# Streaming-encoder layer with PEER on one core: expert weights kept in PSUM by halves of a down tile, a row block's norm spread over the next block's rows, the second pair's first tile computed in one go

## The reference

```python
# e_idx, gates: (1024 tokens, 8 heads, 16 chosen experts)
def block(args):
    hb, eb, gb = args
    u = jnp.take(expert_down, eb, axis=0)
    act = jax.nn.gelu(jnp.einsum('td,thkd->thk', hb, u))
    wv = gb * act
    vv = jnp.take(expert_up, eb, axis=0)
    return jnp.einsum('thk,thkd->td', wv, vv)
x = x + peer_layer(...)
out = rms_norm(x, g_final)
```

## Time and profile before

| what | value |
|---|---|
| median of 3 runs | 2916.48 us (2912.46 to 2918.59) |
| the profiled execution | 2923.75 us |
| its span, first to last instruction | 2921.7 us |
| mean granted PE clock over the span | 0.984 |
| stage with the expert pairs, from the span's start | about 1127 us to the end |
| PE busy in the span | 2785.8 us |
| DVE busy in the span | 2406.7 us |
| POOL busy in the span | 2116.6 us |
| ACT busy in the span | 935.6 us |
| moved by DMA | 717.87 MB |

### The profile page before, as it was taken

How to read it: one execution, slowest core, us unless ns; L and a number is a source line. 1 busy time by engine, 2 the same in 40 slices (tenths; PEclk the granted TensorE clock), 3 DMA queues, 4 the chain that set the end, 5 groups by cost and what they waited for, 6 DMA issues and landing times.

```text
span 2921.7 us, 39464 instructions
## 1 busy us (share of the span) xinstructions
PE 2785.8 (95%) x14843; PEld 2420.2 (83%) x14843; DVE 2406.7 (82%) x4433; ACT 935.6 (32%) x1366; POOL 2116.6 (72%) x1542
## 2 busy tenths in 40 slices
PE   8999999989997999999999999999999999999995
PEld 6688777677887888889989988999888889988995
DVE  2622797654799995889999999998999999999998
ACT  4422443323322995222222222222222222222222
POOL 5444477385686997788778886888777688878885
PEclk9999999999998999999999999999999999999998
DMA  4123422123322778889989988999889799989996
GB/s 154 49 87 99 162 61 84 44 87 108 104 90 102 236 234 283 314 327 349 337 310 352 348 307 322 346 337 351 313 318 344 283 347 346 329 317 348 337 343 218
DMA packets 267725, 717.87 MB, mean 246 GB/s; under 512 B 20880, under 2 KB 104208, under 8 KB 267536
## 3 DMA queue, kind: packets, MB, share of 16 engines
q0 software_dynamic: 110912, 403.75, 36.8%
q1 hardware_dynamic: 156624, 311.61, 31.7%
HBM read 657.86 MB, written 57.41 MB: 245 GB/s over the span
## 4 chain that ended last, share of the span: by engine, by line
DVE 20%; PE 20%; DMA 7%; issue 7%; POOL 5%; ACT 1%; DVEq 0%; POOLq 0%; SPq 0%; ACTq 0%
DVE acc L1883 9%; DVE e_y L1939 4%; DMA up<-in_down,e_idx 4%; PE ybank L1728 3%; PE abank L1712 3%; PE abank L1713 3%; PE abank L1714 3%; PE ybank L1729 3%; PE ybank L1730 3%; DVE up L1871 3%; DMA up<-in_up,e_idx 3%; POOL tdown_lo L1660 2%; DVE w_lo L1932 2%; POOL up L1653 2%; DVE w L1928 2%
## 5 line engine op out<-in xcount | busy, mean ns | idle before, releaser
L1712 PE MATMUL abank<-m_hT,tdown_hi 128*128 128x384 f32 (+1 forms) x1856 | 577.3, 311 | 4.7 <-PEq L1359 2.5
L1714 PE MATMUL abank<-m_hT,tdown_lo 128*128 128x384 f32 (+1 forms) x1856 | 577.5, 311 | 0.0
L1713 PE MATMUL abank<-m_hlo,tdown_hi 128*128 128x384 f32 (+1 forms) x1856 | 576.7, 311 | 0.0
L1728 PE MATMUL ybank<-tup_hi,w_hi 128*128 128x512 f32 x1280 | 506.8, 396 | 46.4 <-DVE e_y L1939 29.0
L941 POOL TENSOR_TENSOR m_wlo<-m_raw,m_whi 128x1024 fp32r<-128x1024 f32 x128 | 312.4, 2448 | 306.7 <-ACT m_whi L719 303.2
L1883 DVE SCALAR_TENSOR_TENSOR acc<-up,e_act,acc 128x1024 f32<-128x1024 f32 x381 | 489.5, 1285 | 43.7 <-DMA up<-in_up,e_idx 16.4
L1871 DVE CUSTOM_DVE_ANT_0 up<-up,acc 128x1024 f32<-128x1024 f32 x384 | 453.1, 1212 | 71.7 <-DMA up<-in_down,e_idx 62.4
L1729 PE MATMUL ybank<-tup_lo,w_hi 128*128 128x512 f32 x1280 | 504.5, 394 | 0.0
L1730 PE MATMUL ybank<-tup_hi,w_lo 128*128 128x512 f32 x1280 | 504.1, 394 | 0.0
L1653 POOL DMA_INDIRECT up<-in_up,e_idx x384 | 396.6, 1033 | 106.7 <-issue 88.9
L1653 POOL DMA_INDIRECT up<-in_down,e_idx x384 | 402.3, 1048 | 98.0 <-issue 73.7
(11 more groups left out here) (241 smaller groups left out, 4566.9 us busy)
## 6 DMA issues: line engine op xcount, KB each, us to landing
e_tup<-in_up SPq DMA_DIRECT2D x128, 512.0 KB
m_raw<-in_tiles SPq DMA_DIRECT2D x116, 512.0 KB, 3.5
e_tdown<-in_downT SPq DMA_DIRECT2D x116, 512.0 KB
gates<-all_table SPq DMA_DIRECT2D x64, 640.0 KB
all_table<-t_out SPq DMA_DIRECT2D x9, 4096.0 KB, 14.7
m_raw<-in_downT SPq DMA_DIRECT2D x12, 512.0 KB, 3.7
up<-in_down,e_idx POOLq DMA_INDIRECT x384
up<-in_up,e_idx POOLq DMA_INDIRECT x384
```

The source lines that it names most:

```text
L1712: nc.tensor.matmul(out, tdown_hi[:, q, at], h2T_hi[:, k, a:b], start=k == 0, stop=False)
L1713: nc.tensor.matmul(out, tdown_hi[:, q, at], h2T_lo[:, a:b, at], start=False, stop=False)
L1714: ins = nc.tensor.matmul(out, tdown_lo[:, q, at], h2T_hi[:, k, a:b], start=False, stop=k == KD - 1)
L1728: nc.tensor.matmul(out, w_hi[r][:, q, ts], tup_hi[r][:, q, ds], start=q == 0, stop=False)
```

## The change

Four things, all in the expert stage.

1. **Weights in PSUM, by halves.** For all pairs but the first, gelu writes back into `abank`, the gates are multiplied there, and `w_hi` and `w_lo` are made from there. `expert_gelu`, `weights`, `weights_high` and `weights_rest` each take one half (256 or 384 columns) at a time: twice as many instructions. A half of `abank` is then free only after `weights_rest`, so `down_half` waits on `w_low` of the same half of the tile before. The queues of ACT and DVE are written anew around the halves. Of the tiles made ahead, gelu reads `w` and writes `abank`.
2. **The tiles made ahead are loaded early.** `w` is used by nothing else now, so `load_pre` waits for the gelu of the tiles made ahead before (ten pairs back), not for `w_low` of the pair before.
3. **The norm of a gathered block, spread.** After the block's last row DVE does only `x2 += acc` and the sum of squares; the mean goes behind the next row, the root on ACT behind 3 rows, the reciprocal behind 5, the scaling behind 7. The third block's norm stays in one piece. The sum of squares writes its products into the row's own slot of the ring, not into `acc`.
4. **First pairs.** down(1,0,0) and down(1,0,1) both stand before up(0,0); up(0,1) has no down tile ahead of it.

The diff, cut to its core:

```diff
+def halves(p, q, half=1):
+    return 2 * (2 * p + q) + half + 1
...
+        def down_out(half):
+            return abank[:, half, 0:(SPLIT[half][1] - SPLIT[half][0]) * P]
+        def weight_place(p, q, half):
+            return down_out(half) if p else w[:, q, SPLIT[half][0] * P:SPLIT[half][1] * P]
...
             def load_pre(p, q):
-                sp.wait_ge(w_low, 2 * (p - 1) + q + 1)
+                read = PRE.index(p) and PRE[PRE.index(p) - 1]
+                sp.wait_ge(gl_ready if read else w_low, halves(read, q))
...
                 if half == 0:
                     pe.wait_ge(down_low, 2 * normal(p) + q + 1)
-                    if q:
-                        pe.wait_ge(gl_ready, 2 * p + 1)
-                    elif p:
-                        pe.wait_ge(gl_ready, 2 * (p - 2 if p - 1 in PRE else p - 1) + 2)
+                if (p, q) == (0, 1) or (p, q) == (1, 0):
+                    pe.wait_ge(gl_ready, halves(0, 1 - q, half))
+                elif p:
+                    pe.wait_ge(w_low, halves(p, q, half) - 2)
...
-                    if p + 1 < NPAIR and t < 4:
+                    if p == 0 and t == 0:
+                        for half in range(2):
+                            down_half(1, 0, half)
+                    elif p + 1 < NPAIR and t < 4 and (p, t) != (0, 1):
                         down_half(p + 1, t // 2, t % 2)
                     up_product(p, t)
...
-                for half, (a, b) in enumerate(SPLIT):
-                    ins = nc.scalar.activation(w[:, q, a * P:b * P], abank[:, half, 0:(b - a) * P], ACT.Gelu_apprx_tanh)
-                ins.then_inc(gl_ready, 1)
+                    act.wait_ge(a_ready, halves(normal(p), q, half))
+                nc.scalar.activation(dst, src, ACT.Gelu_apprx_tanh).then_inc(gl_ready, 1)
...
+                a, b, c, d, e = parts(rows_of_pair(p), (2, 3, 3, 1, 1))
+                up_high_of(p + 1, 0)
+                expert_gelu(p + 1, 0, 0)
                 row_events(a)
+                weights_high(p + 1, 0, 0)
+                row_events(b)
+                expert_gelu(p + 1, 0, 1)
                 if p + 2 < NPAIR:
                     down_high_of(p + 2, 0)
+                up_high_of(p + 1, 1)
+                weights_high(p + 1, 0, 1)
...
+            def row_and_norm(n):
+                row(n)
+                for b in range(DB - 1):
+                    since = n - row_at("up", b, NSEL - 1)
+                    if since == VAR_BEHIND:
+                        dve.wait_ge(row_used, row_at("up", b, NSEL - 1) + 1)
+                        norm_start(slice(ND, ND + 1))
+                    if since == RINV_BEHIND:
+                        norm_root(b, slice(ND, ND + 1))
+                    if since == APPLY_BEHIND:
+                        apply_block(b)
...
-                by = w[:, q].rearrange("p (c t) -> p c t", t=TC)
-                nc.vector.tensor_tensor(by, by, gates[p % 2][:, :, q], ALU.mult).then_inc(w_ready, 1)
+                by = weight_place(p, q, half).rearrange("p (c t) -> p c t", t=TC)
+                nc.vector.tensor_tensor(by, by, gates[p % 2][:, a * P // TC:b * P // TC, q], ALU.mult).then_inc(w_ready, 1)
...
-                a, b, c, d, e = parts(rows_of_pair(p), (3, 2, 1, 3, 1))
+                a, b, c, d, e, f, g = parts(rows_of_pair(p), (2, 1, 2, 1, 2, 1, 1))
```

More of the change, by code:

```diff
@@ L1434 @@
 RU = 8
+VAR_BEHIND, ROOT_BEHIND, RINV_BEHIND, APPLY_BEHIND = 1, 3, 5, 7
 LAST_ROOTS = ((0, 1, 2), (3, 4))
@@ L1714, in down_half @@
                     ins = nc.tensor.matmul(out, tdown_lo[:, q, at], h2T_hi[:, k, a:b], start=False, stop=k == KD - 1)
-                if half == 1:
-                    ins.then_inc(a_ready, 1)
+                ins.then_inc(a_ready, 1)
             def up_product(p, t):
                 if t == 0:
-                    pe.wait_ge(w_low, 2 * (p + 1))
+                    pe.wait_ge(w_low, halves(p, 1))
                     pe.wait_ge(up_low, 2 * (p + 1))
@@ L1795, in row_events @@
                         nc.scalar.activation(act_of[:, b], act_of[:, b], ACT.Gelu_apprx_tanh).then_inc(dots_act, 1)
-                    if kind == "up" and k == NSEL - 1:
-                        if b + 1 < DB:
-                            keep_h2(b + 1)
-                        root(b, slice(ND, ND + 1))
+                    if kind == "up" and k == NSEL - 1 and b + 1 < DB:
+                        keep_h2(b + 1)
+                    for done in range(DB - 1):
+                        if n == row_at("up", done, NSEL - 1) + ROOT_BEHIND:
+                            root(done, slice(ND, ND + 1))
             down_high_of(0, 1)
@@ L1882, in row @@
                     dve.wait_ge(row_used, n)
[L1883 to L1886 removed]
+                    ins = nc.vector.scalar_tensor_tensor(out=acc[:], in0=src, scalar=act_of[:, b, k:k + 1], in1=acc[:],
+                                                         op0=ALU.mult, op1=ALU.add)
+                    if k < NSEL - 1:
+                        ins.then_inc(row_used, 1)
+                    else:
+                        link(ins)
+                        add_block(b)
+                        nc.vector.tensor_tensor_reduce(out=src, in0=x2[:], in1=x2[:], scale=1.0, scalar=0.0, op0=ALU.mult,
+                                                       op1=ALU.add, accum_out=stat[:, 0, ND:ND + 1]).then_inc(row_used, 1)
+            def row_and_norm(n):
[9 more added lines that the diff above has]
+                        apply_block(b)
+                if n + 1 == NROW:
+                    dve.wait_ge(row_used, NROW)
+                    norm_start(slice(ND, ND + 1))
+                    norm_root(DB, slice(ND, ND + 1))
+                    apply_block(DB - 1)
             def norm_start(at):
@@ L1979, in _ @@
                 for n in rows:
-                    row(n)
+                    row_and_norm(n)
                 add_y(p, t)
```

136 lines of the change are left out of this document (65 added, 71 removed).

## The result

| | before | after |
|---|---|---|
| median, first comparison | 2916.05 us (4 runs, 2912.46 to 2918.59) | 2896.61 us (4 runs, 2894.26 to 2900.47) |
| ratio | | 0.9936, 95% interval 0.9918 to 0.9953 |
| ratio in a later comparison (after: 2895.12 us, 6 runs) | | 0.9925, 0.9910 to 0.9939 |
| profiled execution, its span | 2923.75, 2921.7 us | 2894.26, 2892.3 us |
| PE, DVE, POOL, ACT busy | 2785.8, 2406.7, 2116.6, 935.6 us | 2780.3, 2319.9, 2041.9, 966.7 us |

The change is faster by 0.6 to 0.8%, about 20 us, where 47 were forecast; 2870 and its range (2856 to 2889) were missed, and the direction was right. One execution of the kernel before, in the later comparison, took 10435 us at a granted clock of 0.54; the ratios are of the fast runs, without it.

What follows compares the result with a forecast made beforehand. PE's pace was taken to bound the expert stage, with DVE level and its extra work idling PE. About 61 us lost less 15.5 left, 45.5, plus 1.6 at the end: 47 off 2916.5, given as 2870 us, range 2856 to 2889.

Steps and rivals of the forecast that it cites:

- Weights in PSUM: DVE's multiplies and low parts: collisions with POOL go, 328.3 us become 243, 85 us less DVE work.
- The wait for the load of the tiles: ACT at the tiles made ahead: its 14.8 us wait goes, not counted separately from the idle times.
- So at PE's pace nothing waits: Down products' new wait on the low part: one pair laid out, least slack 3.4 us, so no wait.
- Short pairs: Pairs around those made ahead: 1 us of PE idle time left at each of five places, 5 us.
- Block ends: Norms at ends of blocks 0 and 1: 0.5 and 3.5 us of PE's time left, some clock included.
- First pairs and end: Start of the expert stage gains 4.3 us with clock; the last pair, where DVE starts on time, gains 1.6.
- The start of the sum: Expert stage before the last pair: about 61 us lost now, with the gain taken off the median 2916.5.
- The collisions stay: Rival, DVE's weights: PSUM doesn't end collisions with POOL, or costs as much; 3 us gained, 2913; chance 0.07.
- DMA becomes the bound: Rival, expert stage: rows come late after each hindrance, half the idle times stay; gain 25, 2891; chance 0.14.
- The new wait binds: Rival, down(p+1,1,1) waiting on the low part: ACT's high part comes late, 16 us slower, 2932; chance 0.04.
- Everything goes: Rival, expert stage: only 5.5 us of loss at the first pairs stay, 2859; chance 0.15.

Runs made afterwards that it cites:

- feed_pre: Kernel after, with POOL's gathers four rows further ahead and loads of tiles made ahead one pair sooner, before the gates' load: 2865.46 us, ratio 0.9821.
- sbuf_halves: Kernel after, with the weights of all pairs in SBUF, same halves and queues: 2934.76 us, ratio 1.0055 to the kernel before.
- pre_first: Kernel after, with loads of the tiles made ahead one pair sooner in SP's queue, before the gates' load: 2884.23 us, ratio 0.9888.
- feed_ahead: Kernel after, with POOL's gathers four rows further ahead in its queue, past its own subtractions: 2877.69 us, ratio 0.9864.
- feed_pre_small: Kernel after, with gathers four rows further ahead, earlier loads of tiles made ahead, and the norm's one-column products with a scalar operand: 2863.21 us, ratio 0.9811.
- before_feed: Kernel before, with POOL's gathers four rows further ahead in its queue: 2929.75 us, ratio 1.0043.

## Why the prediction was right in kind and wrong in size

The kind of gain was right: the collisions went and PE waits less. Two steps of it failed. The wait for the tiles made ahead was said to go and stayed, and DVE's rows were laid out as if every gather had landed in time. With both mended (feed_pre) 4.9 us of the 34.2 us of delay are left.

**Weights in PSUM: right.** Collisions gone, 328.3 to 254.0 us where 243 were forecast. The term was 11 us too low: some 7 because two halves take 428 + 560 = 988 ns (multiply) and 418 + 551 = 969 (low part), not 947, and the rest because the first pair, still in SBUF, takes 7.3 us with its one collision. An estimate by the Trainium skill's figures in "VectorE: DVE Perf Modes", section "The TRN2 errata — SBUF-src ops pay a fixed extra latency per instruction", was 917; the trace lies further up still. Against the 74 us that were won this is small, and sbuf_halves, slower than the kernel before, shows that the sign of the whole change hangs on PSUM.

**"The wait for the load of the tiles ... goes, since it was issued only after the pair before and is now issued ten pairs ahead": this step failed.** I read the semaphore that the diff changed, not the queue in which it stands. SP issues in the order of its queue (1761.46, 1770.02, 1770.40 above), and the load stands behind `load_gates(p + 3)`, which waits for the gate multiplies of pair p + 1. So the relaxed wait was not the last one, and ACT waited 14.7 us as before. Price: 10.9 us by pre_first.

**"So at PE's pace nothing waits": wrong, since one input of the layout was missing.** I laid out DVE's rows as if each had landed when its turn came. They hadn't: POOL's gathers stand in its queue behind its subtractions, these wait for ACT's copies of tiles, and in the new queue of ACT those stand behind more waiting steps. POOL's wait for `tdown_hi` is 153.6 us now, 86.9 before; in feed_ahead, with the same queue of ACT, 81.7. Pair 23 shows the chain in the kernel after (ACT, POOL, POOL, DVE, PE):

```profile
1775.15 0.39 ACT L1791 ACTIVATE abank<-w 128x256 f32<-128x256 f32 x1 [3.17 <-DMA w<-all_pre]
...
1777.93 2.42 POOL L1677 TENSOR_TENSOR tdown_lo<-e_tdown,tdown_hi 128x1024 fp32r<-128x1024 f32 x1 [2.37 <-ACT tdown_hi L1771]
1780.49 0.96 POOL L1670 DMA_INDIRECT up<-in_down,e_idx  x1
...
1788.37 1.22 DVE L1895 CUSTOM_DVE_ANT_0 up<-up,acc 128x1024 f32<-128x1024 f32 x1 [4.51 <-DMA up<-in_down,e_idx]
...
1791.79 0.50 PE L1745 MATMUL ybank<-tup_hi,w_hi 128*128 128x512 f32 x1 [2.87 <-DVE w_lo L1978]
```

The late load delays ACT's gelu, the gelu the copy that is queued behind it, the copy POOL's subtraction, the subtraction the gather, the gather DVE's row, and the row the low part for which PE stops. (The gather also took long, 7.9 us from issue to landing where the median is 6.5.) In pre_first this stop, 4.6 us of delay in the second profile, is gone. It costs twice, as the window behind it shows (columns as in the earlier trace rows):

```profile
1789.00:1797.00 8.00, 5.21 (x17) 4.29 (x18) 8.00 (x16) 2.10 (x4) 6.91 (x6) 0.79 0.98 369
```

The granted clock is 0.79, so part of these 8 us is at 1.2 GHz instead of 2.4. Before the change the same pair had the collision of 3.37 us instead, and DVE waited only 0.5 us for gathers around it. That is where the expected gain went: DVE, being faster, met its gathers before they had landed. Price: 17.4 us by feed_ahead, of which up to 3 may be collisions of the norm. What the late gathers cost before the change isn't shown.

**Short pairs, "1 us at each of five places": mis-sized** by the two steps above: 18.1 us are left instead of 5. Neither edit alone clears them (8.4 across these pairs in feed_ahead, 5.7 in pre_first, of 8.9); with both (feed_pre) none of these stretches has over 0.6.

**Block ends: mis-sized.** Forecast 0.5 and 3.5 with 1 for the clock, measured 2.5 and 10.5. Late gathers and the late load have most of it (feed_pre: under 0.6 and 3.7), and the one-input products take the 3.7 down to 1.1 (feed_pre_small). That last part I left out: the norm's instructions have two inputs in SBUF and collide as the weights did. I took "5.5 us of work" from the end of block 0, where its products happened to be undisturbed (0.16 us each) and the sum of squares was held up only a little (1.86 us; 1.23 at the end of block 1). After, the sum of squares took 2.45 us there, a one-column product 2.13 and the scaling 2.26 instead of 1.28. The Trainium skill, "SBUF — State Buffer", section "SBUF: two separate sides", says that a DVE instruction with two SBUF inputs and a GpSimd one that reads SBUF exclude each other for the whole instruction. The trace agrees, down to the single column.

**First pairs and end: nearly right.** 4.1 us alone against 4.3, but 2.7 in the changed kernel; the end 2.3 against 1.6.

**The start of the sum.** I counted 61 us lost from a profile 7 us over the median and took the gain off the median. Seen again, the kernel before has 6 us less delay, but the loss behind the first pairs (51.7) agrees with what I had for it, 61 - (4.7 + 2.35 + 1.7) = 52; the surplus of that profile and what my count of idle time and clock missed of it cancelled. So all of the error, but for about 1 us at either end, is in what stays: 34.2 instead of 10.

**The rivals.** "The collisions stay": none of the 504 instructions had one. "DMA becomes the bound": no, in feed_ahead PE was busy for 200 of 200 us with DMA at 0.95. Its time, 2891, was the nearest of all, by luck: rows did come late, but from the place of the gathers in POOL's queue and not from a limit of the transfers. "The new wait binds": 3.6 us, 5 times, where I had none, and in feed_pre it is gone. "Everything goes": this is nearly what feed_pre and feed_pre_small are, 2865 and 2863.

What stays open: how much of DVE's wait for gathers each of ACT's moved steps causes. No run restores ACT's order alone. sbuf_halves has the new queues too: POOL waits 144.8 us for `tdown_hi` there, but the slower DVE only 14.8 for gathers (12.5 + 2.3). So the new queues go with POOL's longer wait, and it reaches DVE only when DVE is fast.

## What to carry to other kernels

When a diff relaxes a wait, look for the last wait ahead of the instruction in its own queue, not for the one that was edited. When an engine is made faster, list what it will now be early for: here its waits for gathers grew from 79 to 131 us and became idle time of PE, and the cure for them (gather four rows sooner) loses 12 us before the change and gains 17 behind it, so it can't be tried beforehand and dropped. Moving one operand of a two-input DVE operation to PSUM was worth 39 us against the same queues with it in SBUF.

## What was not expected of the hardware

- A DVE product of one column, with two SBUF inputs, took 2.13 and 2.84 us (kernel after) and 2.85 (feed_pre) where a POOL subtraction of 1024 columns ran beside it, 0.16 alone; with a scalar operand 0.21 to 0.22, with or without POOL's subtraction beside it.
- With the 640-column operations from SBUF split into 256 and 384 and the queues changed with them (sbuf_halves), all of them together took 440.3 us instead of 328.3, though at the shortest time of each group they would take some 244. The place in the queue counts too: before_feed, with the 256 whole operations, has 391.0 (196.2 + 194.8). How much of it is the splitting alone isn't shown.
- The instruction that is recorded as the first to start can be the one that waits. At the end of block 1 DVE's product is recorded from 2323.80, 0.47 us before POOL's subtraction (2324.27), during POOL's gather instruction, and it ends with the subtraction; the collision of the earlier trace rows has the same order, 0.28 us apart.
- At best the low part of 256 columns took 411 ns with an input in PSUM and 408 from SBUF, the multiply 420 and 410: PSUM shows hardly a price at this size.
